# First stage of a two-block transformer kernel: x loaded with tokens on partitions and turned by TensorE with the RMS roots on the diagonal

## The chip, the cores and the metric

The kernel runs on one core of one Trainium2 chip. The metric is the device time of one execution in microseconds. The core has five engines with an instruction queue each: TensorE (PE, products; PEld are its weight loads), VectorE (DVE), ScalarE (ACT), GpSimd (POOL) and SyncE (SP), which here only issues DMAs. They wait for each other by semaphores.

## The reference, cut to what matters

One sequence of 512 tokens with width 1024 goes through two blocks (a stick-breaking and a latent attention; then a gated delta rule, a forgetting attention and a gated MLP), all in float32. The change is in the very start of the first block, and in an input of the second that is projected early:

```python
def rmsnorm(x, g):
    xf = x.astype(jnp.float32)
    y = xf * lax.rsqrt(jnp.mean(xf * xf, axis=-1, keepdims=True) + EPS)
    return (y * g.astype(jnp.float32)).astype(x.dtype)
...
        mod = c @ w_ada[l] + b_ada[l]
        shift, scale, gate = jnp.split(mod, 3, axis=-1)
        h = rmsnorm(x, norm_gain[l]) * (1.0 + scale[:, None, :]) + shift[:, None, :]
        proj = h @ w_in[l]
        (sb_q, sb_k, sb_v, sb_z, c_q, c_kv, k_rot, mla_z, g_a, g_b) = jnp.split(proj, SPLIT_POINTS, axis=-1)
```

rope turns pairs of columns by position times frequency; its sines and cosines are computed in the kernel ("the angles") and first used after `kr`, well behind the first attention head.

## The kernel before, in words

Activations lie with features on partitions: x is `xT`, eight blocks of 128 features x 512 tokens. Every float32 product is made from three products of rounded halves: a value v is split into hi = round(v) (ScalarE, `copy`, signal HI or WHI) and lo = v - hi (VectorE, `low` or `conv`, signal LO or WLO), and TensorE adds hi*lo, lo*hi and hi*hi (`mm3`). The weights come in chunks of 512 KB into three buffers `raw`; `conv(name, idx, look)` splits, on ScalarE and on VectorE, all chunks up to `look` behind the one named into four slots `whi`/`wlo`. A slot is free when the chunk four before it is used up, a raw buffer when its chunk is split.

The order of work is written out by hand, one function for each engine (`sync_program`, `pool_program`, `tensor_program`, `scalar_program`, `vector_program`), and each engine goes through its list in order. The first stage:

- SyncE loads cst, vec, rcf (constants), x in eight pieces, pf, three weight chunks, eight of the sixteen chunks of `w_ada` (512 KB each, buffers `adab`).
- ScalarE squares each block of x; TensorE sums the squares over partitions by eight products with the ones matrix (line 743); ScalarE makes the root, and VectorE multiplies all of xT by it (line 1788, `xT<-xT,rsb`).
- "pp", a projection of pf for the second block, is the first real work of TensorE: 8 outputs of 2 x 3 products. ScalarE copies them to `zs`.
- The modulation of block b: VectorE takes two dot products of c with 128 rows of `w_ada` (`ada`, line 1799), adds bias and gain (signal MODS), ScalarE makes tmpf = xT * scale + shift (line 1372) and its high half `hhi`, VectorE the low half `hlo`.
- TensorE runs "sbq" as a group (`project_group`): four outputs side by side, block by block, so that it follows the modulation; block b is 4 x 3 products. Then "sbk" (four outputs, 24 products each), "sbv" (4 chunks of 24), the first head `sb_qk(0)` and "cq".
- GpSimd computes the angles at the start (lines 566 to 588, 24 operations on 128x512) and clears parts of `qp` behind `ROPE`; ScalarE makes sine and cosine behind the modulation, with a table load before and after (1376 to 1382), and waits for them before it copies `qp`.

Of the kernel before, what the change touches and what calls it, by code (L numbers as in the profile page):

```python
# [11 lines left out]
ALU = mybir.AluOpType  # L12
# [4 lines left out]
D = 1024  # L17
NB = D // 128
# [151 lines left out]
def build(nc, w_all, cst_d, rc_d, gc_d, rm_d, vec_d, x_d, c_d, pos_d, ada_d, p_d, out_d):  # L170
# [15 lines left out]
    with top:  # L186
# [19 lines left out]
        sb(top, "pad", [128, 32])  # L206
# [10 lines left out]
        with ExitStack() as tmp:  # L217
            rcf = sb(tmp, "rcf", [128, NRC])
# [11 lines left out]
        with ExitStack() as pre:  # L230
# [7 lines left out]
            rk = sb(pre, "rk", [128, S])  # L238
        with ExitStack() as s1:
# [80 lines left out]
        KD = [tmpf[:, 0, :], tmpf[:, 1, :], fPT5[:, 0, :], fPT5[:, 1, :]]  # L320
        KDEC, VBN = gq[:, 4:8, :], gq[:, 8:12, :]
# [67 lines left out]
        XIN = [sig(f"d_x{b}", step=16) for b in range(NB)]  # L389
        XBACK = [sig(f"d_xx{b}", step=16) for b in range(NB)]  # L390
        RAWIN = [sig(f"d_raw{r}", range(r, len(PLAN), NRAW), 16) for r in range(NRAW)]
        ADAIN = [sig(f"d_ada{r}", (r, r + 8), 16) for r in range(8)]
# [27 lines left out]
        XSQ, XSS, XR = (sig(n, range(NB)) for n in ("act_xsq", "pe_xss", "dve_xr"))  # L420
# [70 lines left out]
        def sync_program(e):  # L491
# [17 lines left out]
            def load_ada(n):  # L509
                if n >= 8:  # L510
                    S_.wait_ge(*ADA(n - 8))
                e.dma_start(adab[:, n % 8, :], ada_rows(n)).then_inc(ADAIN[n % 8].sem, 16)

            e.dma_start(cst[:, :], cst_d).then_inc(CST.sem, 16)
            e.dma_start(vec[:, :], vec_d).then_inc(VEC.sem, 16)
            e.dma_start(rcf[:, :], rc_d).then_inc(RCF.sem, 16)
            for b in range(NB):
                e.dma_start(xT[:, b, :], x_d[b * 128:b * 128 + 128, :]).then_inc(XIN[b].sem, 16)
            e.dma_start(pf[:, :, :], p_d.rearrange("(a p) n -> p a n", p=128)).then_inc(PIN.sem, 16)
            load(3)  # L520
            for n in range(8):
                load_ada(n)
            load(6)
            for m in range(8):
                S_.wait_ge(*ZPLE(m))
                e.dma_start(ple[128 * m:128 * m + 128, :], zs[:, m, :]).then_inc(PLST.sem, 16)
            for n in range(8, 14):
                load_ada(n)
            load(9)
            for n in range(14, 16):  # L530
                load_ada(n)
# [10 lines left out]
        def pool_program(e):  # L542
# [19 lines left out]
            e.dma_start(cbt[:, :], c_d.to_broadcast([128, D])).then_inc(CIN.sem, 16)  # L562
# [29 lines left out]
            for r in range(2):  # L592
                if r:
                    G.wait_ge(*QZERO(0))
# [1989 lines left out]
```

## Time and profile before

| | us |
|---|---|
| median of 3 runs (1263.62 to 1265.51) | 1265.44 |
| the profiled execution | 1264.05 |
| its span | 1262.2 |
| TensorE busy, share of the span | 1198.6 (95%) |
| VectorE, ScalarE, GpSimd busy | 711.4, 504.9, 90.8 |
| TensorE in the chain that ended last | 80% |
| mean granted clock of TensorE | 0.987 |

The profile is of one execution. Busy is the time in which an engine has an instruction at work. PEclk is the clock that TensorE was granted as a share of 2.4 GHz; 0.50 is 1.2 GHz. The chain is followed back from the last instruction, at each step to what released it. A float32 product that is not made of halves stands in the trace as two records.

### The profile page before, as it was taken

What the parts mean: (1) busy time and instruction counts of PE and PEld (TensorE: products, weight loads), DVE (VectorE), ACT (ScalarE), POOL (GpSimd) and SP (SyncE); (2) the same over time, 40 slices, a digit from 0 to 9 for tenths busy, and PEclk for the clock granted to TensorE, in tenths of its full rate; (3) what the DMA queues carried; (4) which work ended last, traced back from release to release, by engine and by line L of the source; (5) the groups of instructions that cost most, each with busy time, mean ns of one, the idle gap of its engine ahead of it and who ended that gap; (6) DMA issues with size and microseconds to landing.
All of it is one profiled execution on the core that took longest, in us unless ns stands there. A gap on an engine that the chain in (4) does not pass through costs nothing.

```text
span 1262.2 us, 15880 instructions
## 1 busy us (share of the span) xinstructions
PE 1198.6 (95%) x6480; PEld 959.7 (76%) x6480; DVE 711.4 (56%) x1101; ACT 504.9 (40%) x803; POOL 90.8 (7%) x71
## 2 busy tenths in 40 slices
PE   3699999999999999999999989999999999999996
PEld 1578777877777688787777789878888888888885
DVE  3852465446755676564888685474444444433346
ACT  3461443453453444423435645253322233322244
POOL 7410010101300010000000010000000000000000
PEclk8799999999999999999999999999999999999999
DMA  8823233212221242331221201022222222333322
GB/s 310 284 75 108 72 108 117 67 54 85 69 66 53 65 151 96 119 102 53 79 68 51 67 3 36 1 100 100 101 100 101 97 89 99 125 99 106 105 83 84
DMA packets 36248, 118.21 MB, mean 94 GB/s; under 512 B 4000, under 2 KB 6304, under 8 KB 36176
## 3 DMA queue, kind: packets, MB, share of 16 engines
q1 hardware_dynamic: 34304, 112.15, 26.5%
q0 software_dynamic: 1328, 4.52, 1.2%
q8 instruction: 51, 0.84, 0.3%
q10 hardware_dynamic: 544, 0.52, 0.1%
q14 instruction: 21, 0.17, 0.0%
HBM read 112.99 MB, written 4.19 MB: 93 GB/s over the span
## 4 chain that ended last, share of the span: by engine, by line
PE 80%; DVE 11%; ACT 6%; issue 2%; DMA 1%; POOL 0%; SPq 0%; DVEq 0%; ACTq 0%
PE pb L641 78%; DVE wlo L1788 2%; DVE xT L1788 1%; ACT fP L1508 1%; PE pb L727 1%; ACT mP L1508 1%; PE pb L743 1%; ACT whi L1318 1%; PE pb L887 1%; DVE mnm L2012 1%; DMA xT<-x_d 1%; DVE gq L1791 1%; DVE junk L1799 1%; DVE fP L2026 1%; ACT Y L1318 1%
## 5 line engine op out<-in xcount | busy, mean ns | idle before, releaser
L641 PE MATMUL pb<-hhi,wlo 128*128 128x512 f32 (+2 forms) x1056 | 411.4, 390 | 8.6 <-DVE wlo L1788 6.5
L641 PE MATMUL pb<-hlo,whi 128*128 128x512 f32 (+2 forms) x1056 | 409.5, 394 | 9.6 <-DVE wlo L1788 6.5
L641 PE MATMUL pb<-hhi,whi 128*128 128x512 f32 (+2 forms) x1056 | 410.6, 389 | 0.0
L1788 DVE TENSOR_TENSOR wlo<-raw,whi 128x1024 fp32r<-128x1024 f32 (+1 forms) x178 | 216.8, 1224 | 106.4 <-ACT whi L1318 105.0
L641 PEld LDWEIGHTS pb<-hlo,whi 128*128 128x128 f32 (+1 forms) x1056 | 198.4, 188 | 58.0 <-DVE wlo L1788 10.5
L641 PEld LDWEIGHTS pb<-hhi,wlo 128*128 128x128 f32 (+1 forms) x1056 | 198.5, 188 | 51.7 <-DVE wlo L1788 8.2
L641 PEld LDWEIGHTS pb<-hhi,whi 128*128 128x128 f32 (+1 forms) x1056 | 198.5, 188 | 41.6
L1318 ACT ACTIVATE whi<-raw 128x1024 fp32r<-128x1024 f32 (+1 forms) x178 | 181.1, 1034 | 74.6 <-PE pb L641 68.8
L641 PE MATMUL pb<-alo,whi 128*128 128x512 f32 x176 | 68.5, 389 | 0.0
L641 PE MATMUL pb<-ahi,wlo 128*128 128x512 f32 x176 | 68.5, 389 | 0.0
L641 PE MATMUL pb<-ahi,whi 128*128 128x512 f32 x176 | 68.5, 389 | 0.0
L1318 ACT ACTIVATE ahi<-tmpf 128x512 fp32r<-128x512 f32 x22 | 13.9, 632 | 100.9 <-DVE tmpf L1788 100.9
L1318 ACT ACTIVATE hhi<-xT,vec 128x512 fp32r<-128x512 f32 x16 | 11.6, 725 | 85.8 <-DVE xT L1788 85.8
L1788 DVE TENSOR_TENSOR xT<-xT,pb 128x512 f32<-128x512 f32 x16 | 10.9, 684 | 57.1 <-PE pb L641 57.1
L1788 DVE TENSOR_TENSOR tmpf<-pb,rsb 128x512 f32<-128x512 f32 (+1 forms) x31 | 20.9, 674 | 34.2 <-PE pb L641 29.2
L1726 ACT ACTIVATE tmpf<-tmpf 128x512 f32<-128x512 f32 x22 | 13.9, 632 | 63.9 <-DVE tmpf L1788 63.9
L641 PEld LDWEIGHTS pb<-alo,whi 128*128 128x128 f32 x176 | 33.0, 188 | 6.9
L641 PEld LDWEIGHTS pb<-ahi,wlo 128*128 128x128 f32 x176 | 33.0, 188 | 6.9
L641 PEld LDWEIGHTS pb<-ahi,whi 128*128 128x128 f32 x176 | 33.0, 188 | 6.7
L1788 DVE TENSOR_TENSOR sq<-pb,rsb 128x512 f32<-128x512 f32 x22 | 15.2, 692 | 39.4 <-PE pb L641 39.4
L560 POOL TENSOR_TENSOR spl<-sp,sph 128x896 fp32r<-128x896 f32 x8 | 18.8, 2346 | 163.7 <-ACT sph L1318 163.7
L1508 ACT ACTIVATE mP<-pb,mnm 128x512 f32<-128x512 f32 (+3 forms) x32 | 16.4, 527 | 33.3 <-DVE mnm L1992 33.3
(355 smaller groups left out, 1631.6 us busy)
## 6 DMA issues: line engine op xcount, KB each, us to landing
raw<-w_all SPq DMA_DIRECT2D x173, 512.0 KB, 3.5
adab<-ada_d SPq DMA_DIRECT2D x16, 512.0 KB, 8.8
raw<-w_all SPq DMA_DIRECT2D x10, 384.0 KB, 3.0
xT<-x_d SPq DMA_DIRECT2D x8, 256.0 KB, 7.7
ple_scratch<-zs SPq DMA_DIRECT2D x8, 256.0 KB, 3.1
xT<-x_d POOLq DMA_DIRECT2D x8, 256.0 KB, 3.1
out_d<-xT SPq DMA_DIRECT2D x6, 256.0 KB, 2.3
plr<-ple_scratch POOLq DMA_DIRECT2D x4, 256.0 KB, 3.7
```

The costliest lines, as they stand in the source:

```text
L560: e.tensor_tensor(spl[:, 0:896], sp[:, h % 2, 0:896], fr(sph[:, 0:896]), ALU.subtract).then_inc(SBLO0.sem, 1)
L641: return e.matmul(out, lhs, rhs, start=start, stop=stop, skip_group_check=True)
L727: t = e.matmul(PB[b][:, :], ones, src, start=True, stop=more is None)
L743: e.matmul(PB[7][:, :], ones, sq[:, b % 2, :], start=b == 0, stop=b == 7).then_inc(XSS.sem, 1)
L887: t = e.transpose(PB[b][:, o + 128 * (qi - kb):o + 128 * (qi - kb) + 128], P[:, PO[qi] + 128 * kb:PO[qi] + 128 * kb + 128], ident)
L1318: return e.activation(out, in_, ACT.Copy, **kw)
L1508: t = e.activation(d, src, ACT.Exp, bias=nm[:, i, qi:qi + 1], accum_out=rs[:, i, qi:qi + 1])
L1726: e.activation(tmpf[:, j % 2, :], tmpf[:, j % 2, :], ACT.Silu).then_inc(SG.sem, 1)
L1788: return e.tensor_tensor(out, a, b, op)
L1791: return e.scalar_tensor_tensor(out, a, s, b, op0, op1)
L1799: e.tensor_tensor_reduce(out=junk[:, :], in0=w, in1=cbt[:, :], scale=1.0, scalar=0.0, op0=ALU.mult, op1=ALU.add, accum_out=mod[:, at:at + ...
L2012: t = e.tensor_reduce(mnm[:, h % 2, qi:qi + 1], src, AX.X, ALU.max)
```

## The change

- **x**: a second input `xn_d` holds x as it is, tokens on partitions. It is loaded in four pieces of 128 tokens x 1024 features into the memory of xT. The sums of squares come from ScalarE's accumulator, one for each token (`rsx`, 128x4), as do the roots. VectorE multiplies the identity by them (`turn`, four diagonal matrices), and TensorE computes for feature block b and token block t xn[t, b]^T times the diagonal of t: the block of x with features on partitions, with the root in it, in PSUM banks 4 to 7. Blocks 0 to 3 are turned ahead of pp, blocks 4 to 7 between the blocks 1 to 4 of sbq.
- **Modulation** reads those banks, twice: once into tmpf, once rounded into hhi. `w_ada` has twelve buffers instead of eight (four lie in `gbt`), and SyncE issues fourteen of sixteen chunks ahead of the ple stores.
- **Queues**: cst, vec and pf are issued by ScalarE, rcf and posi by GpSimd behind the last modulation (MODS(7)).
- **Moved behind**: the memsets of qp and then the angles to behind MODS(7); the sines to behind the split of sbv's weights; the constants' casts on VectorE to behind sbk; the sign of the sine and the waits for both to sbv.

The core of the diff:

```diff
+        xn = xT[:, :, :].rearrange("p a b -> p (a b)").rearrange("p (a b) -> p a b", a=4)
+        turn = ssq[:, :].rearrange("p (a b) -> p a b", a=4)
+        def ada_slot(n):
+            r = n % 12
+            return adab[:, r, :] if r < 8 else gbt[:, 2 * r - 16:2 * r - 14, :].rearrange("p a b -> p (a b)")
...
         def sync_program(e):
             def load_ada(n):
-                if n >= 8:
-                    S_.wait_ge(*ADA(n - 8))
+                if n >= 12:
+                    S_.wait_ge(*ADA(n - 12))
-            e.dma_start(cst[:, :], cst_d).then_inc(CST.sem, 16)
-            e.dma_start(vec[:, :], vec_d).then_inc(VEC.sem, 16)
-            e.dma_start(rcf[:, :], rc_d).then_inc(RCF.sem, 16)
-            for b in range(NB):
-                e.dma_start(xT[:, b, :], x_d[b * 128:b * 128 + 128, :]).then_inc(XIN[b].sem, 16)
-            e.dma_start(pf[:, :, :], p_d.rearrange("(a p) n -> p a n", p=128)).then_inc(PIN.sem, 16)
+            for t_ in range(4):
+                e.dma_start(xn[:, t_, :], xn_d[128 * t_:128 * t_ + 128, :]).then_inc(XIN[t_].sem, 16)
             load(3)
-            for n in range(8):
+            for n in range(4):
                 load_ada(n)
             load(6)
+            for n in range(4, 14):
+                load_ada(n)
+            load(7)
+            for n in range(14, 16):
+                load_ada(n)
+            load(9)
             for m in range(8):
                 S_.wait_ge(*ZPLE(m))
                 e.dma_start(ple[128 * m:128 * m + 128, :], zs[:, m, :]).then_inc(PLST.sem, 16)
...
         def pool_program(e):
+            G.wait_ge(*MODS(7))
+            e.dma_start(rcf[:, :], rc_d).then_inc(RCF.sem, 16)
             e.dma_start(posi[:, :], pos_d.to_broadcast([128, S])).then_inc(POS.sem, 16)
+            G.wait_ge(*proj("pp", 1, 3))
...
         def tensor_program(e):
-            T.wait_ge(*CST())
-            for b in range(NB):
-                T.wait_ge(*XSQ(b))
-                e.matmul(PB[7][:, :], ones, sq[:, b % 2, :], start=b == 0, stop=b == 7).then_inc(XSS.sem, 1)
-            free[7] = [RSQ(("x", "ln"))]
+            def turn_x(b):
+                T.wait_ge(*DIAG())
+                bank(4 + b % 4)
+                for t_ in range(4):
+                    t = mm(PB[4 + b % 4][:, 128 * t_:128 * t_ + 128], xn[:, t_, 128 * b:128 * b + 128], turn[:, t_, :],
+                           True, True)
+                t.then_inc(XTR.sem, 1)
+                free[4 + b % 4] = [HI(("1", b))]
+            for b in range(4):
+                turn_x(b)
...
-            project_group([("sbq", i, 128, i) for i in range(4)], h1)
+            project_group([("sbq", i, 128, i) for i in range(4)], h1, between=lambda k: turn_x(k + 3) if 0 < k < 5 else None)
...
         def scalar_program(e):
+            e.dma_start(cst[:, :], cst_d).then_inc(CST.sem, 16)
+            e.dma_start(vec[:, :], vec_d).then_inc(VEC.sem, 16)
+            e.dma_start(pf[:, :, :], p_d.rearrange("(a p) n -> p a n", p=128)).then_inc(PIN.sem, 16)
             e.preload_act_table_set(EXPLN)
+            for t_ in range(4):
+                A.wait_ge(*XIN[t_]())
+                if t_ > 1:
+                    A.wait_ge(*XSQ(t_ - 2))
+                e.activation((sq, tmpf)[t_ % 2][:, :, :].rearrange("p a b -> p (a b)"), xn[:, t_, :], ACT.Square,
+                             accum_out=rsx[:, t_:t_ + 1]).then_inc(XSQ.sem, 1)
...
+            def modulated(b):
+                A.wait_ge(*XTR(b))
+                A.wait_ge(*MODS(b))
+                if b > 1:
+                    A.wait_ge(*LO(("1", b - 2)))
+                for out in (tmpf[:, b % 2, :], hhi[:, b, :]):
+                    t = e.activation(out, PB[4 + b % 4][:, :], ACT.Identity, scale=sc8[:, b:b + 1], bias=mod[:, b:b + 1])
+                t.then_inc(HI.sem, 1)
...
         def vector_program(e):
+            V.wait_ge(*RSQ(("x", "exp")))
+            for t_ in range(4):
+                t = e.tensor_scalar(turn[:, t_, :], ident, rsx[:, t_:t_ + 1], None, ALU.mult)
+            t.then_inc(DIAG.sem, 1)
...
-            V.wait_ge(*RSQ(("x", "exp")))
-            for b in range(NB):
-                tt(xT[:, b, :], xT[:, b, :], rsb[:, :], ALU.mult).then_inc(XR.sem, 1)
...
             for c in range(4):
                 conv("sbv", c)
+                if c == 1:
+                    V.wait_ge(*TRIG("sin"))
+                    e.tensor_scalar(sink[:, :], sink[:, :], cst[:, O_COL + 1:O_COL + 2], None, ALU.mult).then_inc(ROPE.sem, 1)
+                    V.wait_ge(*TRIG("cos"))
```

How this stands in the queues. VectorE before, from the program's start up to the split of the first weights (`junk<-adab` is a dot product of the modulation):

```order
L1826 CAST bcst<-cst 128x128
L1829 CAST bcst<-rcf 128x128 x3
L1830 CAST rcst<-cst 128x128
L1831 CAST rcst<-cst 128x128
L1832 CAST rcst<-cst 128x128
...
L1788 TENSOR_TENSOR xT<-xT,rsb 128x512 x8
L1788 TENSOR_TENSOR plo<-pf,phi 128x512 x2
L1788 TENSOR_TENSOR wlo<-raw,whi 128x1024 x3
L1848 TENSOR_SCALAR sc<-vec 128x8
L1799 ISA junk,mod<-adab,cbt 128x1024
```

And after (`ssq<-cst,rsx` are the four diagonals, `hlo` is the low half of block 0, the three `wlo` behind it are sbq1 to sbq3):

```order
L1845 TENSOR_SCALAR sc<-vec 128x8
L1851 TENSOR_SCALAR ssq<-cst,rsx 128x128 x4
L1803 TENSOR_TENSOR plo<-pf,phi 128x512 x2
L1803 TENSOR_TENSOR wlo<-raw,whi 128x1024 x2
L1814 ISA junk,mod<-adab,cbt 128x1024
...
L1803 TENSOR_TENSOR wlo<-raw,whi 128x1024
...
L1803 TENSOR_TENSOR hlo<-tmpf,hhi 128x512
L1803 TENSOR_TENSOR wlo<-raw,whi 128x1024 x3
```

The constants and the eight multiplications are gone from ahead of the first weights, and one weight chunk (sbq0) stands behind the first modulation.

ScalarE before, behind pp and the modulation of block 7 (the table loads frame sine and cosine; `qp` is the copy of sbq):

```order
L1318 ACTIVATE hhi<-tmpf 128x512
L1376 ACT_TABLE_LOAD
L1378 ACTIVATE sink<-ang 128x512
L1379 ACTIVATE rn<-ang 128x512
L1381 ACTIVATE cosk<-rn,epsc 128x512
L1382 ACT_TABLE_LOAD
L1318 ACTIVATE whi<-raw 128x1024 x2
L1318 ACTIVATE qp<-pb 64x512 x8
L1318 ACTIVATE whi<-raw 128x1024 x7
```

And after:

```order
L1380 ACTIVATE hhi<-pb,mod,sc 128x512
L1330 ACTIVATE whi<-raw 128x1024 x2
L1330 ACTIVATE qp<-pb 64x512 x8
L1330 ACTIVATE whi<-raw 128x1024 x6
L1403 ACT_TABLE_LOAD
L1405 ACTIVATE sink<-ang 128x512
L1406 ACTIVATE rn<-ang 128x512
L1408 ACTIVATE cosk<-rn,epsc 128x512
L1409 ACT_TABLE_LOAD
L1330 ACTIVATE whi<-raw 128x1024
```

The sines moved past eight weight chunks and the copy of sbq; one chunk (cq0) stands behind them.

## Rows read from the trace of the kernel before

**Rows 1.** Chain that ended last, first 130 us: start us, us, what.
```profile
2.12 7.19 DMA xT<-x_d
...
10.11 9.48 PE pb L743 x16
...
20.99 8.28 DVE xT L1788 x8
...
33.15 13.33 PE pb L641 x48
...
55.79 23.28 PE pb L641 x88
...
83.06 46.38 PE pb L641 x204
```

**Rows 2.** Windows, whole core: stretch, its us, busy us by engine, PEclk, DMA, GB/s.
```profile
0.00:10.00 10.00, 0.00 (x0) 0.00 (x0) 1.17 (x12) 1.95 (x3) 2.28 (x8) 1.00 0.82 254
...
12.00:14.00 2.00, 2.00 (x4) 0.84 (x3) 0.00 (x0) 0.68 (x2) 1.83 (x3) 1.00 1.06 415
...
24.00:25.00 1.00, 0.00 (x0) 0.00 (x0) 1.00 (x3) 0.84 (x1) 0.92 (x2) 0.52 1.06 434
...
50.00:52.00 2.00, 0.00 (x0) 0.00 (x0) 1.82 (x7) 0.00 (x0) 0.00 (x0) 0.84 1.02 377
...
61.00:62.00 1.00, 1.00 (x4) 0.78 (x4) 1.00 (x2) 0.97 (x2) 0.00 (x0) 0.70 1.03 410
```

**Rows 3.** Instructions on tile xT, 0 to 40 us: their DMAs.
```profile
DMA to landing us min/median/max: 7.2/7.7/7.8
```

**Rows 4.** Groups by form, ScalarE, whole span: busy us, mean ns, idle before.
```profile
L1318 ACT ACTIVATE whi<-raw 128x1024 fp32r<-128x1024 f32 x165 | 171.1, 1049 | 72.2 <-PE pb L641 66.4 <-DMA raw<-w_all 5.8
...
L1691 ACT ACTIVATION_READ_ACCUMULATOR sq<-pb 128x1 f32 x16 | 3.3, 208 | 0.0
...
L1694 ACT ACTIVATE rso<-rso,epsc 128x4 f32<-128x4 f32 x4 | 1.2, 297 | 0.1
...
L1372 ACT ACTIVATE tmpf<-xT,mod,sc 128x512 f32<-128x512 f32 x8 | 6.5, 812 | 14.6 <-DVE sc L1791 14.6
```

**Rows 5.** Groups by form, VectorE, whole span.
```profile
L2002 DVE TENSOR_SCALAR mP<-mP,mrs 128x128 f32<-128x128 f32 x8 | 2.3, 281 | 0.0
```

**Rows 6.** Timeline of VectorE: start us, us, instruction [idle before, releaser].
```profile
30.81 6.07 DVE L1788 TENSOR_TENSOR wlo<-raw,whi 128x1024 fp32r<-128x1024 f32 x3
...
48.49 0.69 DVE L1788 TENSOR_TENSOR hlo<-tmpf,hhi 128x512 fp32r<-128x512 f32 x1 [3.02 <-ACT hhi L1318]
...
54.51 3.50 DVE L1788 TENSOR_TENSOR wlo<-raw,whi 128x1024 fp32r<-128x1024 f32 x3 [1.89 <-ACT whi L1318]
...
60.64 0.21 DVE L1791 SCALAR_TENSOR_TENSOR sc<-mod,sc,vec 128x1 f32<-128x1 f32 x1
...
64.08 0.21 DVE L1791 SCALAR_TENSOR_TENSOR sc<-mod,sc,vec 128x1 f32<-128x1 f32 x1
```

**Rows 7.** Timeline of TensorE, sbq (63 to 67 us) and the first head (143 us).
```profile
63.93 0.39 PE L641 MATMUL pb<-hhi,wlo 128*128 128x512 f32 x1
...
66.65 0.39 PE L641 MATMUL pb<-hhi,wlo 128*128 128x512 f32 x1
...
143.51 1.05 PE L641 MATMUL pb<-sp,cst 128*128 128x128 f32 x8
```

**Rows 8.** Windows round the angle chain (GpSimd) and the sines (ScalarE).
```profile
9.00:45.40 36.40, 21.72 (x61) 13.14 (x62) 24.02 (x26) 14.08 (x22) 34.39 (x23) 0.81 0.77 290
...
76.16:80.69 4.53, 4.25 (x19) 3.19 (x17) 1.18 (x2) 4.45 (x6) 1.96 (x2) 1.00 0.00 0
```

**Rows 9.** Timeline of GpSimd, end of the angles and memset of qp.
```profile
35.88 2.34 POOL L583 TENSOR_SCALAR rk<-rn 128x512 f32<-128x512 f32 x1
...
39.88 2.34 POOL L583 TENSOR_SCALAR rk<-rn 128x512 f32<-128x512 f32 x1
...
78.68 3.66 POOL L595 MEMSET qp<- 64x2048 f32 x2 [33.35 <-DVE sink L1864]
```

More of the change, by code:

```diff
@@ L238, in build @@
             rk = sb(pre, "rk", [128, S])
+            rcf = sb(pre, "rcf", [128, NRC])
         with ExitStack() as s1:
@@ L562, in pool_program @@
             e.dma_start(cbt[:, :], c_d.to_broadcast([128, D])).then_inc(CIN.sem, 16)
+            G.wait_ge(*MODS(7))
+            e.dma_start(rcf[:, :], rc_d).then_inc(RCF.sem, 16)
             e.dma_start(posi[:, :], pos_d.to_broadcast([128, S])).then_inc(POS.sem, 16)
+            G.wait_ge(*proj("pp", 1, 3))
+            for r in range(2):
+                if r:
+                    G.wait_ge(*QZERO(0))
+                e.memset(qp[64 - 64 * r:128 - 64 * r, :, :].rearrange("p (m r) n -> p m r n", r=2)[:, :, r, :], 0.0
+                         ).then_inc(QZERO.sem, 1)
             G.wait_ge(*POS())
@@ L693, in project_group @@
                 for k in order:
-                    if between is not None and k == between[0]:
-                        between[1]()
+                    if between is not None:
+                        between(k)
                     if k == order[-1]:
@@ L1382, in scalar_program @@
             e.preload_act_table_set(EXPLN)
-            conv("sbq", 3)
-            A.wait_ge(*ROPE())
-            A.wait_ge(*TRIG("cos"))
-            for m in range(4):
-                A.wait_ge(*proj("sbq", m))
-                for r in range(2):
-                    copy(qp[64 * r:64 * r + 64, 2 * m + r, :], PB[m][64 * r:64 * r + 64, :], scale=0.125
-                         ).then_inc(QPE.sem, 1)
-            for m in range(4):
-                conv("sbk", m)
-            for c in range(4):
+            for c in range(2, 4):
                 conv("sbv", c)
@@ L1822, in sum_in @@
                 tt(dst, dst, src, ALU.add).then_inc(SS.sem, 1)
-            V.wait_ge(*CST())
+            e.memset(epsc[:, 0:1], EPS)
+            e.memset(epsc[:, 1:2], 1.0)
+            e.memset(epsc[:, 2:3], math.log(128 ** -0.5))
+            e.memset(epsc[:, 4:5], EPS * EPS)
+            e.memset(epsc[:, 3:4], math.pi / 2).then_inc(EPSR.sem, 1)
+            V.wait_ge(*VEC())
+            e.tensor_scalar(sc8[:, 0:8], vec[:, V_BA + 8:V_BA + 16], 1.0, None, ALU.add).then_inc(DVS.sem, 1)
+            V.wait_ge(*DVS.tick())
+            V.wait_ge(*CST())
+            V.wait_ge(*RSQ(("x", "exp")))
+            for t_ in range(4):
+                t = e.tensor_scalar(turn[:, t_, :], ident, rsx[:, t_:t_ + 1], None, ALU.mult)
+            t.then_inc(DIAG.sem, 1)
+            for k in range(2):
+                low(("p", k), plo[:, k, :], pf[:, k, :], phi[:, k, :])
+            conv("pp", 1, 0)
+            for b in range(NB):
+                if b == 1:
+                    conv("sbq", 0, 0)
+                if b == 2:
+                    conv("sbq", 3, 0)
+                for n in (2 * b, 2 * b + 1):
+                    V.wait_ge(*ADAIN[n % 12](n))
+                    ada(n, ada_slot(n))
+                V.wait_ge(*ADA(2 * b + 1))
+                tt(mod[:, b:b + 1], mod[:, b:b + 1], vc(V_BA + b), ALU.add)
+                stt(sc8[:, b:b + 1], mod[:, 8 + b:9 + b], sc8[:, b:b + 1], vc(V_NG + b), ALU.add, ALU.mult
+                    ).then_inc(MODS.sem, 1)
+                if b:
+                    low(("1", b - 1), hlo[:, b - 1, :], tmpf[:, (b - 1) % 2, :], hhi[:, b - 1, :])
+            low(("1", 7), hlo[:, 7, :], tmpf[:, 1, :], hhi[:, 7, :])
+            conv("sbq", 3)
+            for m in range(4):
+                conv("sbk", m)
+                V.wait_ge(*proj("sbk", m))
+                e.tensor_copy(kp[:, m, :], PB[4 + m][:, :]).then_inc(KPE.sem, 1)
             e.tensor_copy(bcst[:, 0, :], cb(O_IDENT))
```

107 lines of the change are left out of this document (28 added, 79 removed).

## The prediction

> **What bounds the kernel now.** I read the page's busy shares first, then the chain that ended last, then the first 110 us engine by engine, then windows for the clock. TensorE is busy 95% of the span and 80% of the chain is TensorE (the table above). A start that ends earlier therefore shifts everything behind it, as long as nothing behind has a fixed time. The chain shows where the start loses time [rows 1]: x arrives (2.12 to 9.31), eight products with the ones matrix sum the squares (10.11 to 19.59), VectorE multiplies x by the root (8.28 us), the low halves of the first weights are made, and only at 33.15 does the first projection "pp" (48 products) run; the group "sbq" comes in pieces from 48.5 and ends at about 80.3; from 83.06, the start of "sbk", TensorE runs on without a break of note. So I ask one thing: at what time will sbk start? In the granted clock the reader is to see that the engine is at the lower level (0.50, 1.2 GHz) from 24 us and again from 51.4 us, each time 4.5 to 5 us after its steady work stopped, and back at 2.4 GHz 4.5 to 6 us after it resumed [rows 2]: the pp stage took 13.33 us where 48 products at the full pitch need 10.9 (twelve in 2.72 us, from 63.93 to 66.65 [rows 7], are 0.227 us each).
>
> **Step 1, up to the first pp product (33.15 before).** The new path is x, squares, root, diagonal, turn.
> x: the first 10 us moved 2.54 MB (254 GB/s over 10 us), later the queues move 415 GB/s [rows 2]. x is four transfers of 512 KB (2.10 MB); on the other two queues cst, vec, pf and cbt (324 + 64.5 + 512 + 512 KB, 1.45 MB) run beside it. If all of it goes before x's last byte and the early rate stays, 3.54 MB are there at 10 + 1.0/0.415 = 12.4 us; if x went alone at 415 GB/s from its issue at about 2 us it would be there at 7.2. Before, each x transfer landed 7.2 to 7.8 us after issue [rows 3], in company of the same 1.4 MB. posi and rcf (0.46 MB in short rows) are gone from this stretch, so I take 11.2, near the upper end.
> Squares: ScalarE takes 1.05 us for 128x1024 and 0.21 for reading an accumulator [rows 4]; three of the four lie under the transfer, the last one ends at 12.5. Logarithm and exponential over 128x4 cost 0.30 and less [rows 4]: 13.1. Four diagonals at 0.28 each at most [rows 5], overlapped, 0.8: 13.9. Removed against that are eight products of 0.9 us with their handshake (9.48 us of the chain), the root over 128x512 and the 8.28 us of multiplication [rows 1].
> Turn: a 128x128 product of plain float32 is two records; four of them took 1.05 us to the end of the tail, 0.225 us each in pitch [rows 7]. The sixteen of the first four feature blocks are 3.6 us: TensorE is through at 17.5. phi, plo and the first weights need ScalarE until 15.3 and VectorE until 16.6 (whi 1.05, wlo about 1.2 without GpSimd beside it), so they lie under the turn. pp starts at 17.5: 15.65 us earlier.
>
> **Step 2, pp.** With work on TensorE from 13.9 on without a gap I take the full clock: 48 x 0.227 = 10.9, end at 28.4. That is 2.4 us less than the 13.33 of before.
>
> **Step 3, to the first high half of h.** Before, 46.48 to 48.49, 2.0 us: a zs copy, tmpf, hhi. After, the same copy (0.49) and two activations from PSUM at the 0.81 of the modulation [rows 4]: 2.2 us, 30.6. +0.2. VectorE waits for this in its order (the low half of block 0 stands before weights and modulation of block 2): the 3.02 us idle of before [rows 6] grow to about 7, since VectorE is through with the blocks 0 and 1 by 16.6 + 2 x 2.8 + 1.2 = 23.4. That is why twelve buffers don't bring modulation ahead of pp by more than two blocks, as before.
>
> **Step 4, from there to sbk (48.49 to 83.06 before, 34.57 us).** VectorE: low half 0.65, then the three weight chunks sbq1 to sbq3, of which ScalarE can round the last two only behind block 0: 34.8. TensorE from there: 6 products left of block 0 (1.36), blocks 1 to 4 with a turn of 0.9 each (4 x 3.62), blocks 5 to 7 (3 x 2.72): 24.0, end at 58.8 at full clock. The engine had been nearly idle for 6.4 us by then, so I expect the low clock; its price is taken from pp before, 13.33 less 10.9: 61.2. VectorE's modulation runs at 3.45 us a block (60.64 to 64.08 [rows 6]): the last scale at 34.8 + 3.1 + 5 x 3.45 = 55.1, its high half at 56.8, before TensorE asks for it at 58.5. So TensorE, not VectorE, sets this stage now. sbk's first weights wait for sbq0's last product (58.5 + 0.7), then whi and wlo (1.05 + 1.22 and gaps): 61.5. Before, this wait stood behind two table loads and the sines (4.53 us of ScalarE [rows 8]) and cost 2.64 us. 30.9 us instead of 34.57: -3.7.
> wlo of sbk0 could meet the first GpSimd operations; bounds 1.17 and 2.02 us (three in 3.50 and in 6.07 us [rows 6]), I take the lower because GpSimd is in its memset until about 60. The constants' seven small casts and the sink product lie in VectorE's idle time beside the 5.44 us of products of each sbk chunk (24 x 0.227).
>
> **Step 5, the angles.** They start when MODS(7) is there (55.1), posi has landed and the memsets (3.66 us [rows 9]) are through: about 60. The chain took 36.4 us [rows 8]. VectorE has about 2 us of work in each 5.44 us of the sbk stage, so I expect 33 to 36: ready at 95. If every pair had the pitch of the crowded stretch (35.88 to 39.88, 4.00 us [rows 9]) it would be 8 x 4.0 and 10 around them, 42: 102. ScalarE then needs 3.3 us for the sines and a table load, and 2.3 with VectorE for the weights of cq0, which TensorE wants at 61.5 + 43.5 + 2.6 = 107.6. The deadline is 102, so the cost is nothing, with 7 us to spare and none at the upper bound. All weights of sbv are split before ScalarE waits.
> The Trainium skill (SBUF — State Buffer, section "SBUF: two separate sides") says that VectorE and GpSimd share a port pair as an exclusive lock, held for a whole instruction. The trace agrees: the three wlo from 30.81 on take 2.02 us each beside the angles and those from 54.51 on 1.17 without them [rows 6]. The rule speaks for the removal from the start, and against the new place of the angles; by it alone each GpSimd operation waits at most one VectorE instruction, which is the 102 above.
>
> **The sum.** -15.65 - 2.4 + 0.2 - 3.7 = -21.5. The profiled execution took 1264.05 us (span 1262.2), so 1242.5; the median of the runs shown is 1.4 higher, 1265.44, and from it I predict 1244.
>
> **The rivals.**
> - The clock is low when the turn starts. For: nothing has run on TensorE by 13.9, 3.8 us later than the 10.11 of before. Against: with no product in the first 10 us the granted clock stood at 1.00 [rows 2]. It would cost what the low clock cost pp before, 2.4 us, less what VectorE still needs: 1246. The Trainium skill (TensorE: Matmul & The Clock Gate, section "What's actually happening") calls the throttled state the default which activity releases; the first 10 us of this trace contradict it, and the measurement decides.
> - The clock doesn't fall between pp and sbq, because pairs of products run at 30.6, 32.4 and 33.6. Then the last high half binds (56.8), and sbk starts at 59.8: 1242.
> - The three queues share so that weights and ada rows (3.5 MB issued behind x) arrive with x instead of after it. For: nothing in the trace shows a 512 KB x transfer. Against: the eight x transfers landed 7.2 to 7.8 us after issue [rows 3] with 4 MB behind them on the same queue. x at 10 + 4.5/0.415 = 21 us at most, TensorE 8 us later on average: 1252.
> - The angles are late: posi lands as slowly as at the start (7.1 us) and each pair takes 4.00: 105, 3 us behind the deadline: 1247.
> - Slower than before: the same chain, with its sines between ScalarE, VectorE and everything behind. It decides once the angles come later than 102, and has eaten the whole gain at 102 + 21.5 = 123.5, that is if the GpSimd chain takes 63 us instead of 36.4; every microsecond beyond is lost: 1270 at 68 us. The longest operations recorded, 2.34 [rows 9], make 42 of it, so there is hardly anything for it.
> - The change gives nothing: that would need TensorE to wait at the end of sbq for something of fixed time, 21 us long. The DMA queues could: 8 MB of ada rows at 0.41 MB/us are 20 us, and the last rows are issued behind raw chunk 6 at about 33, landed by 37, wanted at 52. No.
>
> **How the numbers follow.** Forecast 0.62 (own range 1241.5 to 1246.5); clock low at the turn 0.14; clock never falls 0.09; queues share 0.06; angles late 0.05; slower or unchanged 0.04. The range reaches from both clock and transfer falling well (1240) to a late x and late angles (1250.5). A measurement of this kernel can tell about 0.2% (2.5 us) from no change: faster 0.95, within it 0.02, slower 0.03.
>
> **What would show it.** pp's first product at 16 to 19 us and its last near 28; no group of products with the ones matrix; sixteen and then four times four small products of xT with ssq; VectorE idle about 7 us before the first hlo; modulation at 3.45 us a block; first sbk product at 60 to 63; angles ready at 90 to 98; the first cq product right behind the first qp,kp group. From there on all rows stand 21 us earlier and keep their lengths. Wrong would be: x landed after 13; the low clock during pp; TensorE waiting for hhi in blocks 2 to 6 (VectorE or ScalarE sets the pace after all); any idle TensorE of over 1 us between sbk and the first attention head.

## The result and the profile after

The changed kernel takes 1244.68 us (median of 4 runs, 1244.26 to 1244.96), the kernel before 1265.47 in the same series: ratio 0.9837 (95% interval 0.9820 to 0.9854), 20.8 us less. The forecast was 1244.0. The profiled execution is itself the one of 1244.68 us, with a span of 1242.8. The page's busy times; before, TensorE was at 95% and GpSimd worked in the first slices:

```profile
PE 1194.7 (96%) x6528; PEld 963.8 (78%) x6528; DVE 702.3 (57%) x1097; ACT 503.6 (41%) x803; POOL 90.7 (7%) x72
```

The chain of waits up to the first attention head (start, duration, what; compare [rows 1]):

```profile
2.13 10.28 DMA xT<-xn_d
...
14.28 0.89 DVE ssq L1851 x4
...
15.21 16.39 PE pb L647 x80
...
33.59 0.69 DVE hlo L1803
34.28 2.28 DVE wlo L1803 x2
...
36.61 24.08 PE pb L647 x115
...
60.77 1.07 ACT whi L1330
...
61.86 1.24 DVE wlo L1803
...
63.14 46.38 PE pb L647 x204
```

The eight ones-products and the 8.28 us of VectorE are gone; the first TensorE piece holds the turn and pp together and ends at 31.6 instead of 46.5. The group sbk starts at 63.14 instead of 83.06, 19.92 us earlier, and its 204 records take 46.38 us as before. From there to the end of the span it is 1179.66 us, before 1179.14: between these two executions the gain is 19.4 us, all of it ahead of sbk. The 0.5 us more behind sbk are less than what executions with the same work differ by there (last section).

TensorE in the turn (start, duration, line, operation, count, idle before and releaser):

```profile
15.21 5.48 PE L647 MATMUL pb<-ssq,xT 128*128 128x128 f32 x32 [15.21 <-DVE ssq L1851]
20.45 0.48 PE L647 MATMUL pb<-plo,whi 128*128 128x512 f32 x1
```

The sixteen products took 5.24 us up to pp's first, where 3.6 were forecast. The windows of this group alone (stretch, its length, busy time and records, granted clock, DMA share, GB/s):

```profile
15.20:18.70 3.50, 3.49 (x16) 1.00 1.02 408
18.70:20.40 1.70, 1.70 (x17) 1.00 1.03 412
```

Half the records fill 3.5 us, the other half 1.7. That is the ratio of the two levels, 1.2 to 2.4 GHz, yet the column of the granted clock says 1.00 for both. The clock record of the trace begins only at the first change: here that is at 18.7 us, in the kernel before at 13.8, and until then the view fills in 1.00. The row of [rows 2] with 1.00 for the first 10 us was such a filled row. The Trainium skill (TensorE: Matmul & The Clock Gate, section "What's actually happening") calls the throttled state the default; by that rule, the trace agrees: it starts low.

### The profile page after: what moved, and what is told of

Read it like the earlier page. It is cut to its first block, busy times and chain, and to the rows that moved or that the text cites. A ratio compares the mean times of both kernels' runs of the same rounds, so it can differ in the third digit from the quotient of the medians.

```text
span 1242.8 us, 15960 instructions
## 1 busy us (share of the span) xinstructions
PE 1194.7 (96%) x6528; PEld 963.8 (78%) x6528; DVE 702.3 (57%) x1097; ACT 503.6 (41%) x803; POOL 90.7 (7%) x72
## 2 busy tenths in 40 slices
DMA packets 35593, 118.22 MB, mean 95 GB/s; under 512 B 3936, under 2 KB 6112, under 8 KB 35520
## 4 chain that ended last, share of the span: by engine, by line
PE 81%; DVE 10%; ACT 5%; issue 2%; DMA 1%; POOL 0%; SPq 0%; DVEq 0%; ACTq 0%
PE pb L647 79%; DVE wlo L1803 2%; ACT fP L1523 1%; PE pb L733 1%; DVE xT L1803 1%; DMA xT<-xn_d 1%; ACT mP L1523 1%; PE pb L899 1%; DVE mnm L2030 1%; ACT whi L1330 1%; DVE gq L1806 1%; DVE fP L2044 1%; ACT Y L1330 1%; DVE mP L2020 1%; ACT hhi L1330 0%
## 5 line engine op out<-in xcount | busy, mean ns | idle before, releaser
L1803 DVE TENSOR_TENSOR xT<-xT,pb 128x512 f32<-128x512 f32 x16 | 10.9, 684 | 57.1 <-PE pb L647 57.1
```

The lines of the kernel that those rows point to most:

```text
L1803: return e.tensor_tensor(out, a, b, op)
```

## The experiments

All times are medians of 4 runs, each ratio is against the kernel before, run on the same chip. The changed kernel itself has 1244.68 from a series of its own; the one with eight buffers (below), which does the same work in the same order on the engines, gave 1244.66 beside the warm-up, the early modulations and the two queues, so I read medians that differ by more than about 1 us. That is a rule of thumb from one pair: the runs stand in four series, and the kernel before, with the same code in each, has medians of 1265.47, 1265.02 (warm-up, two early modulations, two queues, eight buffers), 1264.14 (angles in front, slower angles, x in the old way, the first combination) and 1265.03 (the rest). A difference across series, and that is any difference from the changed kernel, is therefore open by about 1 us. A single profile says less: those two kernels, equal in time, started sbk at 63.14 and at 64.68 (the last section says where that lies). Each diff is against the changed kernel.

### Warm-up: was the clock low in the turn?

```
+ e.memset(fr(hlo[:, 7, :]), 0.0).then_inc(WARM.sem, 1)     # VectorE, first
+ T.wait_ge(*WARM())
+ for _ in range(48):                                        # result not used
+     mm(PB[7][:, :], hlo[:, 7, 0:128], hlo[:, 7, :], True, True)
  for b in range(4):
      turn_x(b)
```

> The changed kernel with 48 float32r products of a zeroed tile (128x128 by 128x512, bank 7) on TensorE ahead of the turn, from about 1 us on; the rest as it is. Theory A (TensorE stands at the low clock until it has worked, and the profile's 1.00 before 18.7 us is only missing records): the warm-up ends at about 14 to 15 us, the sixteen turned products take 3.6 us instead of 5.24, pp starts 1.6 us earlier (at 18.8) and everything behind too: 1243.1 us. Rival B (the clock was at full speed, as the page shows, and the first products are slow because weights and operands of plain float32 limit them there): the turn still takes 5.2 us, 1244.7 us.

Measured: 1243.47 us (1242.97 to 1244.02), ratio 0.9835 (0.9821 to 0.9850). TensorE, from 8.5 us on (25 of the 48 warm-up products):

```profile
8.71 5.83 PE L648 MATMUL pb<-hlo 128*128 128x512 f32 x25
15.16 3.84 PE L648 MATMUL pb<-ssq,xT 128*128 128x128 f32 x32 [0.63 <-DVE ssq L1856]
18.76 0.48 PE L648 MATMUL pb<-plo,whi 128*128 128x512 f32 x1
```

The turn takes 3.60 us, exactly the forecast's figure, and pp starts 1.69 us earlier: the low clock in the turn is shown. But only 0.23 us of it reach sbk (62.91 against 63.14), so the 1.2 us by which the median is lower are only partly its doing; behind sbk this execution is 1.4 us shorter with the same work. The clock falls behind pp in both: the changed kernel is below 1.00 in 34 to 40 (shown under step 4 below), this one in 32 to 40:

```profile
32.00:34.00 2.00, 0.87 (x3) 0.44 (x4) 2.00 (x3) 2.00 (x3) 0.00 (x0) 0.71 1.03 414
34.00:36.00 2.00, 2.00 (x4) 0.80 (x4) 2.00 (x3) 1.12 (x2) 0.00 (x0) 0.50 1.02 406
36.00:38.00 2.00, 2.00 (x6) 1.54 (x6) 1.85 (x4) 0.00 (x0) 0.00 (x0) 0.50 1.03 414
38.00:40.00 2.00, 2.00 (x10) 1.80 (x9) 1.97 (x6) 1.05 (x2) 0.00 (x0) 0.58 1.02 406
```

At 1.2 GHz for (1 - mean) / 0.5 of each window, that is 6.8 us here and 3.4 there. The longer low stretch can have cost up to 1.7 us of the gain. The kernel with eight buffers (below), profiled in this series, is the better partner, since its low stretch is 6.8 us long too: there pp starts at 21.40 and sbk at 64.68, here at 18.76 and 62.91. Against it 1.8 us reach sbk, and 1.85 us the time of the profiled execution (1243.06 against 1244.91).

### VectorE's 8 us behind block 1: two modulations between the copies of pp

```
  for m in range(8):
+     if m == 2: modulated(0)
-     if m == 4: conv("sbq", 1, 0)
+     if m == 4: conv("sbq", 2, 0)
+     if m == 5: modulated(1)
      ...                     # the copy of pp's m-th piece
- modulated(0)
  conv("sbq", 3, 0)
- for b in range(1, NB):
+ for b in range(2, NB):
      modulated(b)
```

VectorE splits sbq1 behind the modulation of block 2, sbq2 and sbq3 ahead of that of block 3, to match.

> The changed kernel with ScalarE's modulation of blocks 0 and 1 between the zs copies of pp (ahead of copies 2 and 5) instead of behind the last, and the splits of sbq1 to sbq3 on VectorE behind modulation 2 and ahead of 3. Theory A (the 8.1 us idle of VectorE and the 2 us idle of TensorE after pp are only a matter of the order written): the first sbq product follows pp's last at 31.6 instead of 33.6, sbq3's weights are there at 33.9 instead of 37.7, the clock does not fall at 35.8, and sbk starts at 58.5 to 59.5 instead of 63.1: 1240.5 us. Rival B (the ada rows that arrive after 25 us limit VectorE, and TensorE waits for the high halves of blocks 2 to 4 instead): sbk at 62 or later, 1243.5 us or more.

Measured: 1240.17 us (1239.82 to 1242.01), ratio 0.9812 (0.9796 to 0.9828): 4.5 us under the changed kernel, no run of the one inside the range of the other. VectorE in the changed kernel:

```profile
33.59 0.69 DVE L1803 TENSOR_TENSOR hlo<-tmpf,hhi 128x512 fp32r<-128x512 f32 x1 [8.14 <-ACT hhi L1380]
```

and here:

```profile
25.62 0.68 DVE L1806 TENSOR_TENSOR hlo<-tmpf,hhi 128x512 fp32r<-128x512 f32 x1
27.71 1.23 DVE L1817 CUSTOM_DVE_ANT_0 junk<-adab,cbt 128x1024 bf16<-128x1024 f32 x1 [1.41 <-DMA adab<-ada_d]
...
29.94 1.23 DVE L1817 CUSTOM_DVE_ANT_0 junk<-adab,cbt 128x1024 bf16<-128x1024 f32 x1 [1.00 <-DMA adab<-ada_d]
```

The idle 8.14 us are gone. What is left is 2.4 us of waiting for ada rows 4 and 5, which are issued behind weights. The profiled execution is the slowest of the four (1242.01, the others 1239.82 to 1240.25): in it sbk starts at 62.02, 1.1 us earlier, and what follows takes 1.5 us less. So of the 4.5 us of the medians the trace shows 1.1 on the chain; the faster three were not profiled. (Against the kernel with eight buffers, from the same series, it shows 2.7: 64.68 less 62.02.) The time fits theory A, the trace fits rival B as well: the first product of sbq does follow pp at 31.47, but sbk comes at 62.02 and not by 59.5, and the clock still falls: VectorE, held up by rows 4 and 5, is late with sbq's weights. So the order costs time, but how much of the 4.5 us is its doing is not shown. This version has the lowest median of all that were run.

### x on two queues

```
  # SyncE
- for t_ in range(4):
+ for t_ in (0, 2):
      e.dma_start(xn[:, t_, :], ...)
  # ScalarE, ahead of cst, vec and pf
+ for t_ in (1, 3):
+     e.dma_start(xn[:, t_, :], ...)
```

> The changed kernel with x tiles 0 and 2 issued by SyncE and 1 and 3 by ScalarE ahead of cst, vec and pf. Theory A (x landed at 12.4 because the 0.9 MB of cst, vec and pf on ScalarE's queue took turns with it): the last x tile lands at about 10 us, the turn starts at 13, pp at 18 to 18.5 and all behind about 2.2 us earlier: 1242.5 us. Rival B (the total in flight decides, since weights and ada rows then take turns with x2 and x3, or cst and pf come too late): last of x, cst and pf at 12 or later, within 0.5 us of 1244.7 us.

Measured: 1246.01 us (1244.97 to 1246.41), ratio 0.9854 (0.9839 to 0.9869). The expectation of a gain fell, and the time lies above the rival's band too. ScalarE:

```profile
10.49 1.04 ACT L1363 ACTIVATE tmpf<-xT 128x1024 f32<-128x1024 f32 x1
...
17.69 1.15 ACT L1330 ACTIVATE phi<-pf 128x512 fp32r<-128x512 f32 x2 [5.50 <-DMA pf<-p_d]
```

ScalarE squares the last quarter of x at 10.49, 1.9 us earlier. But pf, behind two quarters of x on ScalarE's queue, lands only at 17.6, and the chain begins with

```profile
2.15 11.76 DMA vec<-vec_d
```

since vec is on that queue too, and VectorE reads it ahead of the diagonals. The 1 MB that goes first on the second queue delays what the very next step needs: the roots are there at 12.19, the turn begins only at 15.06, 0.15 us earlier than in the changed kernel. That explains why nothing is gained. It does not explain the 1.3 us lost: pp starts at 21.10 right behind the turn, without a wait for pf, and why sbk starts as late as 66.05 (a low stretch of 6.8 us has part in it) was not taken apart.

### x alone in front

```
  # SyncE: pf behind x;  GpSimd: cbt once x's second quarter is there
+ e.dma_start(pf[:, :, :], ...)          # was on ScalarE's queue
  load(3)
  ...
+ G.wait_ge(*XIN[1]())
  e.dma_start(cbt[:, :], c_d ...)
```

> The changed kernel with pf issued by SyncE behind the four x tiles instead of by ScalarE beside them, and cbt issued by GpSimd only when x tile 1 is there (1.05 MB that no longer take turns with x). Theory A (x landed at 12.4 for the bytes beside it, 3.5 MB in all): the last tile lands at 10 to 10.5, the turn starts at 13, pp at 18.3, all behind 2 us earlier: 1242.7 us. Rival B (pf or cbt now comes too late, as pf did when x was on two queues): phi behind 14.5 or the first dot product behind 19.5, 1244.5 us or more.

Measured: 1242.53 us (1241.29 to 1244.10), ratio 0.9824 (0.9808 to 0.9840), 2.1 us under the changed kernel, where 2.0 were expected. Its chain begins with

```profile
2.11 7.13 DMA xT<-xn_d
```

and its TensorE with

```profile
12.04 6.49 PE L649 MATMUL pb<-ssq,xT 128*128 128x128 f32 x32 [12.04 <-DVE ssq L1852]
18.29 0.48 PE L649 MATMUL pb<-plo,whi 128*128 128x512 f32 x1
```

x lands 3.2 us earlier; the turn takes 6.25 us instead of 5.24, more of it at the low clock; pp starts 2.16 us earlier and sbk 1.2.

### The angles back beside the first stage

```
  # GpSimd: posi loaded and the angle chain (the same 23 operations) at the start
+ e.dma_start(posi[:, :], ...)
+ ...                                    # cast, reduction, eight pairs
  G.wait_ge(*MODS(7))
  e.dma_start(rcf ...)
```

> The changed kernel with the load of posi and the whole angle chain on GpSimd at the start again, ahead of MODS(7); sines, constants and all else stay behind. Theory A (the angles beside the first stage cost time by making VectorE's instructions longer): wlo near 2 us and every second dot product near 2.1 us until the chain ends at about 48; pp's start hardly moves (the turn hides it), VectorE becomes the bound of sbq and sbk starts 2 to 4 us later than 63.1: 1247 to 1249 us. Rival B (VectorE has 8 us idle in this stage and TensorE is the bound of sbq, so longer instructions are hidden): within 0.7 us of 1244.7 us.

Measured: 1252.37 us (1249.97 to 1252.98), ratio 0.9903 (0.9885 to 0.9921): 7.7 us of the 20.8 come from where the angles stand, more than either expectation allowed. VectorE:

```profile
36.57 5.01 DVE L1806 TENSOR_TENSOR wlo<-raw,whi 128x1024 fp32r<-128x1024 f32 x3
...
46.51 1.21 DVE L1817 CUSTOM_DVE_ANT_0 junk<-adab,cbt 128x1024 bf16<-128x1024 f32 x1
...
47.87 2.08 DVE L1817 CUSTOM_DVE_ANT_0 junk<-adab,cbt 128x1024 bf16<-128x1024 f32 x1
```

Three splits take 5.01 us, 3.49 in the changed kernel; every second dot product takes 2.08 instead of 1.23; a block's modulation takes 4.6 us instead of 3.45, and VectorE is the one that TensorE waits for again. sbk starts at 70.76, 7.6 us later than in the changed kernel. Not all of it is VectorE: posi is loaded beside x, which lands 1.06 us later, the diagonals are done another 0.3 us later, and the turn takes 6.19 us instead of 5.24, so pp starts 2.35 us later (22.80). The other 5.3 us arise behind that, where VectorE's longer instructions stand and where the low stretch of the clock is 6.8 us long instead of 3.4. GpSimd's instructions grow as well, one of them far more than the others:

```profile
16.56 5.61 POOL L588 TENSOR_SCALAR rk<-rn 128x512 f32<-128x512 f32 x1
```

The same operation takes 1.49 us at its shortest, and the longest VectorE instruction beside this one takes 1.40. So 2.34 us, from which the prediction took its upper bound for the angles, is not the longest that occurs, and its "at most one VectorE instruction" does not hold here.

### The angles later: how much room is there?

```
+ for _ in range(8):                     # results not used
+     G.wait_ge(*GPS.tick())
+     e.tensor_scalar(rk[:, :], rn[:, :], 2.0, None, ALU.mult)...
```

> The changed kernel with eight more operations (rk from rn, results unused) ahead of the last of the angle chain, 12 to 13 us of GpSimd. Theory A (the angles have about 5 us to spare: cq0's weights are split at about 104, TensorE wants them at 109.3): the angles come at about 111 instead of 98.5 and TensorE waits 7 us ahead of cq0: 1251.5 us. Rival B (the wait is hidden by other work or by the order of the first head, so that the slack is larger): 1244.7 to 1247 us.

Measured: 1252.81 us (1251.60 to 1253.55), ratio 0.9909 (0.9893 to 0.9925). ScalarE at the sines:

```profile
112.57 0.63 ACT L1408 ACTIVATE sink<-ang 128x512 f32<-128x512 f32 x1 [23.43 <-POOL ang L605]
```

The sines come 14.05 us later than in the changed kernel (98.52, below) and 8.1 us are lost: about 6 us of room. The first cq product says 5.1 (109.31 to 118.22 is 8.9). TensorE idled for 7.24 us ahead of it, and the granted clock then stood at 0.50 from 118 to 122 us, so part of the 8.1 us is the low clock and not the wait.

### Twelve buffers or eight

```
- r = n % 12
- return adab[:, r, :] if r < 8 else gbt[...]
+ return adab[:, n % 8, :]
```

> The changed kernel with eight buffers for the rows of w_ada again instead of twelve; SyncE's order stays. Theory A (the four extra buffers buy nothing: VectorE stands on the high half of block 0, rows 8 to 13 only wait for ADA(0) to ADA(5) and still land before they are used): 1244.7 us, modulation still at 3.45 us a block. Rival B (rows 12 and 13 wait for dot products behind 37 us and raw chunk 6 and 7 behind them on the queue land late): sbk's weights late by some us, 1246 to 1250 us.

Measured: 1244.66 us (1244.39 to 1244.98), ratio 0.9844 (0.9827 to 0.9861). The four further buffers are worth nothing measurable. The trace shows the queues of this kernel nearly idle from 36 to 40 us (6 and 8 GB/s), where the changed kernel moves about 400: rows wait for a free buffer, and nobody waits for them. (With twelve buffers all sixteen chunks of `w_ada` are issued ahead of the ple stores, not fourteen: the last two leave at 35.81 us, the stores begin at 38.09.)

### x in the old way, every move kept

x with features on partitions in eight transfers, ones-products, root over 128x512, VectorE's multiplication, eight ada buffers; angles, sines and constants stay behind.

> The changed kernel with the first kernel's way of x only: xT in eight transposed pieces (on SyncE, first in its queue), squares, eight products with the ones matrix, root over 128x512, eight multiplications on VectorE, no turn; eight buffers for the ada rows as in the run of that name; modulation reads xT. Everything moved behind stays behind, cst, vec and pf stay on ScalarE's queue. Theory A (the moves give most of the 20 us, the turn only a few): products with ones end at about 14.5, xT is ready at 21, pp starts at 23.5 at the low clock, sbk at about 68: 1249.7 us. Rival B (the turned path gives at least half): pp at 29 or later, 1255 us or more.

Measured: 1250.49 us (1249.92 to 1250.84), ratio 0.9890 (0.9872 to 0.9908). Its chain:

```profile
18.67 2.86 DVE xT L1793 x5
...
21.69 1.89 DVE xT L1793 x3
...
25.98 13.44 PE pb L644 x48
```

The multiplication that took 8.28 us beside GpSimd [rows 1] takes 4.9 without it. pp starts at 25.98 with TensorE idle for 8.83 us before, and takes 13.44 us (granted clock 0.53 from 20 to 30 us), as before the change. Turning x is worth 5.8 us; the expectation of 1249.7 was met within 0.8, though sbk starts at 71.01 and not at 68.

### Angles in front and the sines ahead of sbk's weights

The kernel with the angles in front, and ScalarE's two table loads and sines ahead of the copy of sbq, as before the change.

> The kernel of x4_angfront (1252.4 us, angles at the start) with the sines, both table loads and the sign of the sine back between the modulation and sbq's copy, where the first kernel had them; turn, order of the rest and constants as in the changed kernel. Theory A (the sines there hold up sbk's first weights by some 2.2 us, 2.64 us of idle TensorE in the first kernel against 0.5): 1254.6 us. Rival B (the sines are hidden behind TensorE's last blocks of sbq): 1252.4 us.

Measured: 1256.37 us (1254.17 to 1258.93), ratio 0.9940 (0.9922 to 0.9957), 4.0 us over the kernel with the angles alone. Its chain:

```profile
67.06 1.28 ACT L1396
68.35 0.63 ACT sink L1398
68.98 0.53 ACT rn L1399
...
70.28 1.28 ACT L1402
71.57 1.06 ACT whi L1333
```

These 4.5 us stood between the last high half and sbk's first weights. TensorE waits 3.61 us ahead of sbk (0.41 with the angles alone), and sbk starts 3.25 us later. That confirms the reading of [rows 8]; the expected 2.2 us were too low.

### Three attempts to combine

Warm-up, two early modulations and ada rows 0 to 7 ahead of weight chunks 3 to 5:

```
  load(3)
- for n in range(4):
+ for n in range(8):
      load_ada(n)
  load(6)
```

> The changed kernel with three edits: the warm-up products, the modulation of blocks 0 and 1 between the zs copies (both as run before, 1243.5 and 1240.2 us), and new, ada rows 4 to 7 issued by SyncE ahead of raw chunks 3 to 5 instead of behind (there VectorE waited 1.4 and 1.0 us for rows 4 and 5, and TensorE 2 us for sbq's weights). Theory A (the three add up): pp at 18.8, first sbq product right behind pp at 30, clock full throughout, sbk at 57 to 58.5: 1237.0 us. Rival B (raw chunks 3 to 5 are now late by the same amount, and TensorE waits for sbq1 to sbq3 at the start of the group): sbk at 60 or later, 1239.5 us.

Measured: 1244.67 us (1243.83 to 1245.10), ratio 0.9845 (0.9830 to 0.9860). Both expected times fell; the rival's mechanism is what happened, and sbk starts at 63.86. ScalarE:

```profile
28.91 1.06 ACT L1334 ACTIVATE whi<-raw 128x1024 fp32r<-128x1024 f32 x1 [3.71 <-DMA raw<-w_all]
```

The weights now land late, and behind this split stand the copies that empty pp's banks: TensorE stood idle for 1.87 and 1.12 us for them. Rows 0 to 5 only, with the same warm-up:

> The changed kernel with the warm-up products, the modulation of blocks 0 and 1 between the zs copies, and ada rows 0 to 5 (not 0 to 7, which made raw chunk 3 late and lost all) issued ahead of raw chunks 3 to 5. Theory A (both waits of the runs before were DMA arrivals, and this order gives each in time: rows 4 and 5 by 25, raw 3 and 4 by 26.7): sbq follows pp at 30, sbq3's weights at 33, sbk at 57 to 58: 1238.7 us. Rival B (the queue is full either way until 40 us and some chunk is always late): sbk at 60 or later, 1241 us or more.

Measured: 1241.89 us (1239.08 to 1243.33), ratio 0.9816 (0.9797 to 0.9834), the rival's side (sbk at 61.84); the split waits 1.34 us for its weights. It is not better than the two early modulations alone. With pf and cbt held back as well, and 38 warm-up products instead of 48:

> The kernel of the run before (x10_order) with, in addition, x ahead of pf and cbt as in x9_xfirst, and 38 instead of 48 warm-up products. Theory A (the gains add up): pp at 17, sbk at 55.5 to 57: 1237.0 us. Rival B (the DMA queue sets when the rows 4 to 7 and raw chunks 3 to 5 land, so an earlier x only makes VectorE wait longer): no better than x10_order within 0.5 us.

Measured: 1240.95 us (1240.69 to 1242.64), ratio 0.9814 (0.9799 to 0.9828): about 4 us over theory A, and 0.9 under the run before. That one's four runs reach from below to above all of these, so the rival is not refuted. ScalarE:

```profile
26.14 1.06 ACT L1336 ACTIVATE whi<-raw 128x1024 fp32r<-128x1024 f32 x1 [3.61 <-DMA raw<-w_all]
```

Single gains of 1.2, 4.5 and 2.1 us came to 3.7 together, no more than the two early modulations give alone. pp starts 2.6 us earlier than without the last step (16.10 against 18.70), but the split that waits for its weights ends at 27.20 against 27.45: the queues move about 410 GB/s without a pause up to there, and what TensorE gained, the transfer did not.

## Why the prediction was right, and where its steps were not

The time was right within 0.7 us. Part of that is luck: between the profiled executions the change moved the span from 1262.2 to 1242.8, 19.4 us, where the sum said 21.5. From the execution whose rows it read, the sum made 1242.5; 1244.68 is 2.1 more, 1.6 in the steps up to sbk and 0.5 behind it. The 1.4 us added for the median of before, which no step of the kernel stands for, covered most of that, and within the steps an error of +3.0 met one of -1.3. Of the prediction's own signs, pp's first product (16 to 19 us) and its last (near 28) were missed, with 20.45 and 31.6; sbk (60 to 63) and the angles (90 to 98) by 0.1 and 0.5. None of the rows came that it had called wrong.

**Step 1 (pp at 17.5; measured 20.45).** Two terms were mis-sized. x landed at 12.4 instead of 11.2: the changed kernel moved 285 GB/s in its first 10 us and 414 after, and pf and cbt, 1 MB, shared it, as holding them back showed (x at 9.24). The turn took 5.24 us instead of 3.60. Here the step that failed is the sentence "the first 10 us of this trace contradict it, and the measurement decides": it was no measurement. The trace of before held the contradiction, in the weight loads of its ones-products, two to a product:

```profile
11.09 0.34 PEld L743 LDWEIGHTS pb<-sq,cst 128*128 128x128 f32 x1 [0.52 <-ACT sq L1346]
11.95 0.34 PEld L743 LDWEIGHTS pb<-sq,cst 128*128 128x128 f32 x1 [0.52 <-issue]
...
14.63 0.30 PEld L743 LDWEIGHTS pb<-sq,cst 128*128 128x128 f32 x2 [0.71 <-ACT sq L1346]
15.53 0.30 PEld L743 LDWEIGHTS pb<-sq,cst 128*128 128x128 f32 x2 [0.60 <-ACT sq L1346]
```

Half a product takes 0.86 us at 11.09, a whole one 0.90 at 14.63. The rival "clock low when the turn starts" was thus true in mechanism, at 1.64 us instead of its 2.4 (about 2 after what VectorE still needed), and it should have been the forecast. Squares, root and diagonals took 2.76 us (2.7).

**Step 2 (10.9).** pp took 11.14, at the full clock. The reason given, that TensorE works up to it without a gap, held, but with less room than it sounds: the clock rose at 18.7, inside the turn and 1.75 us ahead of pp. In the kernel with x in the old way pp took 13.44 with idle time ahead of it.

**Step 3 (2.2; VectorE idle about 7).** 1.97 us, and VectorE idle 8.14 us. The prediction used this wait to argue that twelve buffers bring nothing, which eight buffers confirmed, and left it there. That it costs time went unseen: the wait is one of order, and the kernel that reorders is 4.5 us faster, though its trace shows only a part of that ahead of sbk.

**Step 4 (30.9 us).** 29.6. Modulation ran at the forecast pitch, and TensorE, not VectorE, set the stage. The clock fell, but the low stretch was shorter than before: of these windows

```profile
34.00:36.00 2.00, 0.87 (x4) 0.30 (x2) 2.00 (x3) 2.00 (x3) 0.00 (x0) 0.94 1.03 416
36.00:38.00 2.00, 1.86 (x5) 0.76 (x4) 2.00 (x3) 0.79 (x2) 0.00 (x0) 0.50 1.01 406
38.00:40.00 2.00, 2.00 (x8) 1.59 (x9) 1.86 (x3) 0.00 (x0) 0.00 (x0) 0.71 1.03 397
```

the first says that sbq's first products still ran at the full clock, and by 40 it is back. The price of 2.4 us, taken from pp, was too high for this execution; the low stretch of 3.4 us can cost 1.7 at most. The wait ahead of sbk is about 0.4 us, before 2.64; that term was right, and the kernel with the sines in front shows its cause.

**Step 5 (ready at 95, no cost).** GpSimd's first and last operations:

```profile
58.09 0.56 POOL L569 DMA_DIRECT2D rcf<-rc_d  x1 [56.16 <-DVE sc L1806]
...
59.22 3.67 POOL L576 MEMSET qp<- 64x2048 f32 x2
...
97.87 0.62 POOL L602 TENSOR_SCALAR ang<-ang 128x512 f32<-128x512 f32 x1
```

and ScalarE behind them:

```profile
98.52 0.63 ACT L1405 ACTIVATE sink<-ang 128x512 f32<-128x512 f32 x1 [10.86 <-POOL ang L602]
...
101.74 1.06 ACT L1330 ACTIVATE whi<-raw 128x1024 fp32r<-128x1024 f32 x1
```

The chain took 35.7 us, inside the 33 to 36 expected, but its cast began at 62.85: MODS(7) came 2.7 us later than forecast, and the memset stood between. ScalarE waits 10.86 us and TensorE not at all, since its own work up to cq0 is done at 109.3. The deadline of 102 moved to about 104 with the later sbk; the delayed chain puts it 5 to 6 us behind 98.5.

**The sum.** +2.95 in step 1, +0.2 in step 2, -0.2 in step 3, -1.3 in step 4: sbk at 63.14 instead of 61.5. Behind it, after took 0.5 us longer than before.

**Where the 20.8 us come from**, as far as single undoing shows: angles out of the first stage 7.7, sines out of the way of sbk's weights 4.0, x turned by TensorE 5.8, twelve buffers 0. These make 17.5. All three terms cross series. Taken instead by the ratios to the kernel before in its own series (0.9837 for the change, 0.9903 with the angles in front, 0.9940 with the sines too, 0.9890 with x in the old way) they are about 8.3, 4.7 and 6.7, 19.7 in all. So 1 to 3 us, in constants, queue order and the interplay, are left that were not tried apart.

## What to carry to other kernels

Read the clock from durations of equal products as well as from the clock's row: where an engine has not yet changed state the row may be empty, and a first product at twice its usual time says so. When an engine in program order stands idle behind one early wait, look for work behind the wait that doesn't need it: the kernel with two modulations moved is 4.5 us faster, and then waits for DMAs instead. At a start where the queues are full throughout, gains on the engines don't add: what matters is which megabyte comes first, and every one moved ahead needs a check of what the next step then waits for.

## What the runs showed of the hardware that was not expected

- The early clock: with nothing ahead of it, the longest records of the turn take 582 ns, the first half of them 426 on average and the second 287, and when that changes differs between executions. From a start at 15.21 the turn took 5.24 us, from 15.05 (eight buffers) 6.35, from 12.04 (x alone in front) 6.25; with the warm-up 3.60.
- The low stretch behind pp differed as well with nearly the same work: 3.4 us in the changed kernel, 6.8 with the warm-up, and with eight buffers the clock is back only in the window from 40 to 42. No run explains the difference.
- Behind sbk all kernels but the one with slower angles do the same work, yet the time from sbk's first product to the end of the span was 1178.0 to 1178.4 us in six of the profiled executions and 1179.1 to 1180.3 in seven. In five of these seven (before, after, the angles in front, x alone in front, the last combination) the clock's windows of 30 to 60 us between 740 and 820 us fall to a mean of 0.94 to 0.97; the two other long ones (the first two combinations) have no such fall, so it is not the whole cause. About 1.5 us of any difference between two profiled executions can lie there.
- VectorE beside GpSimd: a split of 128x1024 took 1.16 us alone and 1.67 beside the angles of the kernel with the angles in front; the kernel before had 2.02 [rows 6]. GpSimd's `rk<-rn` over 128x512 took 1.49 us at its shortest, 2.35 in many places, and once 5.61 (the angles in front).
